# Moving the forget term, the third state and the gate of a transformer stage between VectorE, ScalarE and TensorE

## What is computed

```python
# shared_kv: once, from the state after layer 0
h = modulate(rms_norm(x, kv_norm_g), shift, scale)
kvf = h @ kv_w                                   # keys, values, 16 forget logits
k = rms_norm(k, k_norm_g)
dcum = cumsum(log_sigmoid(f_logit))              # [16 heads, 256]
# layer 1
h = modulate(rms_norm(x, pre_mix_g[1]), sh_m, sc_m)
qg = h @ w_qg                                    # q and gate
q = rms_norm(q, q_norm_g); gate = sigmoid(qg[..., 1024:])
logits = q k^T * scale + dcum[t] - dcum[s]       # causal
o = softmax(logits) v
y = (o * gate) @ w_o
```

## Time and profile before

| | |
|---|---|
| median of 3 runs | 1771.63 us (1769.91 to 1776.13) |
| the profiled execution | 1773.06 us, of which its span 1771.3 us |
| TensorE busy | 1724.3 us, 97% of the span |
| VectorE / ScalarE busy | 1149.1 us, 65% / 896.9 us, 51% |
| mean granted TensorE clock | 0.993 |
| bytes moved | 362.93 MB, 205 GB/s mean |

### The profile page before, as it was taken

How to read it: one execution, slowest core, us unless ns; L and a number is a source line. 1 busy time by engine, 2 the same in 40 slices (tenths; PEclk the granted TensorE clock), 3 DMA queues, 4 the chain that set the end, 5 groups by cost and what they waited for, 6 DMA issues and landing times.

```text
span 1771.3 us, 22292 instructions
## 1 busy us (share of the span) xinstructions
PE 1724.3 (97%) x9048; PEld 1436.2 (81%) x9048; DVE 1149.1 (65%) x1600; ACT 896.9 (51%) x1280; POOL 7.7 (0%) x21
## 2 busy tenths in 40 slices
PE   9999999999989999999999989999999999999998
PEld 6897788888767888888889858888888889778887
DVE  5888977788757654655457967554655556675553
ACT  4755544464667444544444566444544355574432
POOL 0000000000000000000000000000000000000000
PEclk9999999999999999999999999999999999999999
DMA  9958677856534655555564325545654565345451
GB/s 387 415 218 322 246 299 290 323 209 260 206 120 177 254 199 178 209 184 177 186 212 152 119 72 187 182 175 190 214 183 169 195 210 221 106 155 187 168 192 48
DMA packets 54840, 362.93 MB, mean 205 GB/s; under 512 B 5825, under 2 KB 9025, under 8 KB 14546
## 3 DMA queue, kind: packets, MB, share of 16 engines
q1 hardware_dynamic: 52978, 350.95, 54.1%
q0 software_dynamic: 1760, 10.56, 1.5%
HBM read 360.43 MB, written 1.05 MB: 204 GB/s over the span
## 4 chain that ended last, share of the span: by engine, by line
PE 77%; DVE 12%; ACT 2%; issue 1%; DMA 0%; DVEq 0%; ACTq 0%
PE pp L634 73%; DVE low L1924 4%; DVE raw L1937 2%; PE pp L909 2%; PE pp L841 1%; DVE hf L2068 1%; ACT wh L1381 1%; PE pp L986 1%; DVE tb L1924 0%; DVE hl L1924 0%; DVE x L1927 0%; DVE Sb L2219 0%; DVE sc L2320 0%; DVE h L1924 0%; DVE top L2317 0%
## 5 line engine op out<-in xcount | busy, mean ns | idle before, releaser
L1924 DVE TENSOR_TENSOR low<-raw,wh 128x2048 fp32r<-128x2048 f32 (+3 forms) x346 | 639.0, 1861 | 363.9 <-ACT wh L1381 363.4
L1381 ACT ACTIVATE wh<-raw 128x2048 fp32r<-128x2048 f32 (+3 forms) x352 | 536.9, 1544 | 421.6 <-PE pp L634 290.8
L634 PE MATMUL pp<-wh,hh 128*128 128x512 f32 x1312 | 521.7, 398 | 5.3 <-ACT hh L1648 2.2
L634 PE MATMUL pp<-low,hh 128*128 128x512 f32 x1312 | 510.1, 390 | 0.6 <-DVE low L1924 0.4
L634 PE MATMUL pp<-wh,hl 128*128 128x512 f32 x1312 | 506.9, 392 | 3.5 <-DVE hl L1924 3.5
L634 PEld LDWEIGHTS pp<-wh,hh 128*128 128x128 f32 x1312 | 247.5, 189 | 63.5 <-issue 11.9
L634 PEld LDWEIGHTS pp<-wh,hl 128*128 128x128 f32 x1312 | 247.2, 189 | 57.1 <-DVE hl L1924 4.7
L634 PEld LDWEIGHTS pp<-low,hh 128*128 128x128 f32 x1312 | 246.6, 188 | 50.1 <-DVE low L1924 1.7
L634 PE MATMUL pp<-wh,hidh 128*128 128x512 f32 x592 | 232.1, 392 | 0.0
L634 PE MATMUL pp<-wh,hidl 128*128 128x512 f32 x592 | 230.6, 389 | 0.0
L634 PE MATMUL pp<-low,hidh 128*128 128x512 f32 x592 | 230.5, 389 | 0.0
(11 more groups left out here) (230 smaller groups left out, 1187.0 us busy)
## 6 DMA issues: line engine op xcount, KB each, us to landing
raw<-in_w SPq DMA_DIRECT2D x300, 1024.0 KB, 4.8
raw<-in_w SPq DMA_DIRECT2D x24, 768.0 KB, 4.3
raw<-in_w SPq DMA_DIRECT2D x13, 512.0 KB, 19.2
firstw<-in_w SPq DMA_DIRECT2D x6, 1024.0 KB, 14.5
gain<-in_w POOLq DMA_DIRECT2D x6, 512.0 KB, 5.1
bT<-in_rel POOLq DMA_DIRECT2D x1, 2048.0 KB, 10.4
cst<-in_csts POOLq DMA_DIRECT2D x1, 1029.0 KB, 10.0
xT<-in_xT SPq DMA_DIRECT2D x1, 1024.0 KB, 5.5
```

The lines of the kernel that those rows point to most:

```text
L634: return e.matmul(out, lhsT, rhs, start=start, stop=stop, skip_group_check=True)
L1381: q.then_inc(e.activation(wh[j % NW][:, c], raw_of(i, kt * n)[:, c], ACT.Copy), s_wh, (j, part))
L1924: return e.tensor_tensor(out, a, b, op)
```

## The change

It does six things, all between the start of `kv_v` 0 and the end of this attention.

1. The high and low part of the forget sum lie in one tile (rows 0-31 and 64-95 high, 32-63 and 96-127 low), so a head needs one matmul of 64 rows instead of two of 32. `dL` and eight `dR` are made on ScalarE (9 instructions) instead of VectorE (10).
2. The third state is made on ScalarE from PSUM (16 instructions of 128 columns) instead of VectorE (8 of 512).
3. The sigmoid becomes exp(min(x,0) - ln(1 + exp(-|x|))): Abs (2), Exp, Ln, Exp on ScalarE, min (2) and a subtraction on VectorE; no change of table. The PSUM pair is released by the second min.
4. Four ada pieces each in three stretches of the stream instead of twelve evenly.
5. One more empty fill call after `q1`, and one after `gate1` (there ScalarE and VectorE have the first part of the sigmoid).
6. Two fill calls a round up to round 7 instead of 4.

```diff
-    marks = [..., (52, 32), (56, 32), (72, 44), (78, 44), (88, 48)]
+    marks = [..., (52, 32), (54, 32), (58, 36), (60, 36), (64, 40), (67, 40), (71, 44), (78, 44), (88, 48)]
...
         def fox_rate(i):
-            return 2 if i < 5 else 1
+            return 2 if i < 8 else 1
...  (TensorE: scores)
-                            rr = slice(32 * (h % 4), 32 * (h % 4) + 32)
-                            for i in range(2):
-                                ins = mm(s_r..., dL[i][rr, 128 * u["qb"]:128 * u["qb"] + 128],
-                                         dR[i][h // 4][rr, 0:nk], False, i == 1)
+                            rr = u["rows"]
+                            ins = mm(s_r..., dL[rr, 128 * u["qb"]:128 * u["qb"] + 128],
+                                     dR[h // 2][rr, 0:nk], False, True)
...  (TensorE: fox_fill)
                 yield from group("q1", 0, h(3), (s_side, ("qk", "q1")), fillp)
                 yield
+                yield
                 head_norm("q1", t_r)
                 yield "second"
-                yield from group("gate1", 0, h(3), (s_gate, ("gate", 1)), fillp)
+                yield from group("gate1", 0, h(3), (s_side, ("gate_min", 1, 1)), fillp)
+                yield
                 yield "own"
...  (ScalarE)
+            def gate_abs(g, ring):
+                _, before = ta.begin(("gate", g), (s_side, ("gate_less", g)))
+                q.wait_ge(*before)
+                q.wait_ge(s_mm, (("gate", "gate1")[g], 0, "end"))
+                for n in range(2):      # 128 x 512 each, PSUM -> a
+                    q.then_inc(e.activation(a[:, t, :], ring...tiles[:, t, :], ACT.Abs), s_sideact, ("gate_abs", g, n))
+            def gate_log(g):            # 128 x 1024 each
+                q.then_inc(e.activation(a, a, ACT.Exp, scale=-1.0), s_sideact, ("gate_exp", g))
+                q.then_inc(e.activation(a, a, ACT.Ln, bias=1.0), s_sideact, ("gate_log", g))
+            def gate_sigmoid(g):
+                q.wait_ge(s_side, ("gate_less", g))
+                q.then_inc(e.activation(o, o, ACT.Exp), s_gate, ("gate", g))
...  (ScalarE: fox_fill)
-                yield from ahead.steps("q1", 0, "T")
+                for n, _ in enumerate(ahead.steps("q1", 0, "T")):
+                    if n == 3:
+                        gate_sigmoid(0)
+                    yield
                 head_squares("q1", fillp)
                 yield
+                yield
                 head_roots("q1", t_r)
                 yield "second"
                 yield from ahead.steps("gate1", 0, "T")
-                gate_sigmoid(1, fillp)
+                gate_abs(1, fillp)
+                gate_log(1)
+                yield
                 waiting("fox", 4, gT)
                 yield "own"
+                gate_sigmoid(1)
...
+            def third_h(m):             # between the pieces of kv_k
+                for c in range(2):
+                    q.wait_ge(s_aux, ("hT", 3, m, c))
+                    for i in range(4):
+                        ins = e.activation(h3[:, m, k, :], misc...[:, 128 * i:128 * i + 128], ACT.Identity, bias=..., scale=...)
+                    q.then_inc(ins, s_h3, ("hf", 3, m, c))
+            def forget_sides():         # after values(("vv", 1)), ahead of group("q", 0)
+                e.activation(dL[:, :], dH[:, :], ACT.Identity, bias=fc[:, 1:2], scale=fc[:, 0:1])
+                for j in range(8):
+                    ins = e.activation(dR[j][:, :], dH[:, :], ACT.Identity, bias=fc[:, 10 + j:11 + j], scale=fc[:, 2 + j:3 + j])
+                q.then_inc(ins, s_sideact, "dR")
-            ahead.group("q", 0)
+            ahead.group("q", 0, upto=1)
             head_squares("q")
             ahead.first("gate", 0)
             head_roots("q")
-            gate_sigmoid(0, pairs)
+            gate_abs(0, pairs)
+            gate_log(0)
...  (VectorE)
+            gate_min(0, pairs) ahead of attention; in fox_fill gate_less(0) before the third call's yield,
+            gate_min(1, fillp) in the new call after gate1, gate_less(1) ahead of lo_of(4, 0..3)
-            ahead.group("kv_k", 0, between=lambda: h_parts(3, 0, *inputs_of("q")))   # and for 1
+            ahead.group("kv_k", 0)
-            q.then_inc(tt(dD[:, :], dT[:, :], dH[:, :], ALU.subtract), s_side, "dD")
-            for i, d in enumerate((dH, dD)):
-                e.tensor_scalar(dL[i][:, :], d[:, :], fc[:, 0:1], fc[:, 1:2], ALU.mult, ALU.add)
-                for j in range(4):
-                    ins = e.tensor_scalar(dR[i][j][:, :], d[:, :], ...)
+            for r in (slice(32, 64), slice(96, 128)):
+                q.then_inc(tt(dH[r, :], dT[r, :], dH[r, :], ALU.subtract), s_side, ("dD", r.start))
```

More of the change, by code:

```diff
@@ L175, in constants @@
     z = np.zeros((128, 128))
-    forget = np.zeros((128, 10))
+    forget = np.zeros((128, 18))
     forget[:, 0] = p % 32 < 16
     forget[:, 1] = p % 32 >= 16
-    for j in range(4):
-        for g in range(4):
-            forget[32 * g + 16 + 4 * j + g, 2 + j] = -1.0
-            forget[32 * g + 4 * j + g, 6 + j] = 1.0
+    for j in range(8):
+        for g in range(2):
+            for part in range(2):
+                forget[64 * g + 32 * part + 16 + 2 * j + g, 2 + j] = -1.0
+                forget[64 * g + 32 * part + 2 * j + g, 10 + j] = 1.0
     made = {"ident": np.eye(128),
@@ L352, in build @@
         lf = [place(f"lf{i}", [128, T], F32, big + 34816 + 1024 * i) for i in range(3)]
-        dH, dD = [place(f"d{n}", [128, T], F32R, big + 34816 + 1024 * i) for i, n in enumerate("HD")]
-        dL = [place(f"dL{i}", [128, T], F32R, big + 33792 - 1024 * i) for i in range(2)]
-        dR = [[place(f"dR{i}{j}", [128, T], F32R, big + o) for j, o in enumerate(places)]
-              for i, places in enumerate(((38912, 39936, 40960, 41984), (36864, 37888, 43008, 44032)))]
+        dH = place("dH", [128, T], F32R, big + 34816)
+        dL = place("dL", [128, T], F32R, big + 33792)
+        dR = [place(f"dR{j}", [128, T], F32R, big + 36864 + 1024 * j) for j in range(8)]
         aq = place("aq", [128, 4, T], F32, big)
@@ L1201, in tensor_program @@
             whole("q", 0, h(3), (s_side, ("qk", "q")))
-            whole("gate", 0, h(3), (s_gate, ("gate", 0)), between=lambda: head_norm("q"))
+            whole("gate", 0, h(3), (s_side, ("gate_min", 0, 1)), between=lambda: head_norm("q"))
             into_attention()
@@ L2256, in lo_of, with gate_min, gate_less @@
                 s_lo.at["h", hv, tile, 0] = s_lo.n
+            def gate_min(g, ring):
+                for n in range(2):
+                    t = slice(2 * n, 2 * n + 2)
+                    q.wait_ge(s_sideact, ("gate_abs", g, n))
+                    q.then_inc(e.tensor_scalar(gT[:, 4 * g + 2 * n:4 * g + 2 * n + 2, :],
+                                               ring.of((("gate", "gate1")[g], 0)).tiles[:, t, :], 0.0, None, ALU.min),
+                               s_side, ("gate_min", g, n))
+            def gate_less(g):
+                o = gT[:, 4 * g:4 * g + 4, :]
+                q.wait_ge(s_sideact, ("gate_log", g))
+                q.wait_ge(s_side, ("gate_min", g, 1))
+                q.then_inc(tt(o, o, ta.of(("gate", g))[:, :, :], ALU.subtract), s_side, ("gate_less", g))
             def split_fox(u):
@@ L2299, in fox_fill @@
             def fox_fill():
-                yield from ahead.steps("q1", 0, "T")
+                for n, _ in enumerate(ahead.steps("q1", 0, "T")):
+                    if n == 2:
+                        gate_less(0)
+                    yield
                 head_begin("q1")
+                yield
                 yield
@@ L2305, in fox_fill @@
                 yield from ahead.steps("gate1", 0, "T")
+                gate_min(1, fillp)
+                yield
+                gate_less(1)
                 for tile in range(4):
@@ L2529, in vector_program @@
             modulated("q")
-            ahead.group("kv_k", 0, between=lambda: h_parts(3, 0, *inputs_of("q")))
+            ahead.group("kv_k", 0)
             head_begin("kv_k0")
-            ahead.group("kv_k", 1, between=lambda: h_parts(3, 1, *inputs_of("q")))
+            ahead.group("kv_k", 1)
             head_begin("kv_k1")
@@ L2560, in vector_program @@
             head_scale("q", qg, qT[:, 0:4, :])
+            gate_min(0, pairs)
             fill = Fill(fox_fill())
```

41 lines of the change are left out of this document (27 added, 14 removed).

## The result

The changed kernel takes **1781.58 us** (median of 4 runs, 1780.88 to 1783.55), the kernel before in the same comparison 1773.06 (1769.91 to 1776.13). The ratio is 1.0045, 95% interval 1.003 to 1.0059: slower by 8 us. The forecast was 1773.5, in a range of 1763 to 1781. What came is the second rival (slower by the clock, 1779), 2.6 us above its price.

The account below looks back on a forecast made before the run. TensorE, busy 97%, was taken as the bound, with VectorE late at `q`. Attention +4.0, ahead of it -4.5 and half clock +1.7 gave net +1.2 on 1773.06, 1774.3, stated as 1773.5 us; range 1763 to 1781.

Parts of the forecast that it names:

- the second rival: Clock falls at all three long waits in attention (norm, round 9, `o`), 1.7 to 2.4 us each: 1779; chance 0.22.
- the price of the clock: In attention: one stretch at half clock counted, given idle stretches of 3.8 us, +1.7 us.
- The sum: Attention 78.0 us (57.3 work, 20.7 losses) against 74.0; ahead of it -4.5; clock +1.7; net +1.2, giving 1774.3.
- Ahead of attention: Before attention: VectorE relieved, `k_scale(0)` at about 420, both waits at `q` go, gate starts earlier: -4.5 us.
- the signs of being wrong: Observations that would refute the forecast: attention of 74 us or less, or a wait for low parts in `kv_k`.
- The stalls: Attention waits: 1.4 at start, 4.0 in rounds 3 to 5, 3.9 around the norm, 3.8 at round 9, 4.6 at `o`.
- The forget term: In attention: half of each four forget matmuls goes, 8 times each, -3.2 us; up to -4.8 if heads' matmuls overlap.
- The sigmoid: In attention: the new chain adds +1.1 us at the start and belongs to the +2.4 us at `o`.
- Rival 1: VectorE and ScalarE keep up, ada43 lands before it is missed, the gain stays: 1762 to 1765, say 1764; chance 0.24.

Follow-up runs that it names:

- The unread products: Changed kernel plus 78 extra matmuls of 256 columns, results unread, in four places where TensorE idles: 1774.08 us, ratio 0.9998 to the kernel before.
- the kernel with the work alone: Changed kernel with all three order edits undone (old ada marks, old rate, no empty steps): 1768.35 us, ratio 0.9966; another session 1769.35, 0.9975.

## Why the prediction was wrong

**The step that failed is the price of the clock.** The sum had "one as well, +1.7". Attention was put at 78.0 + 1.7 = 79.7 us and took 83.7. Split as above, the idle time was 18.3 us (I had 20.7), the work 57.1 (57.3), and the clock took up to 8.4. The unread products settle it: the same order with the clock held took 78.02 us. That is the sum's 78.0, with no fall counted. I had seen three of the places and their size, and had the case as a rival (three falls, 1779), but gave it 0.22. The fourth, the wait of 2.3 us at the turn of round 5, stood in the sum and not among the places where the clock might fall; it fell there as well, and twice as long at `o`. What spoke for it was in the sum itself: it held waits of 2.3, 3.8, 3.9 and 4.6 us where the trace of before had nothing longer than 2.15 in attention. In the changed kernel the clock fell behind every one of these four. The rule of the Trainium skill, "TensorE: Matmul & The Clock Gate", section "HAM oscillation", by which gaps between bursts bring it about each time, holds for these four waits, but not for the kernel before, which kept the clock through 2.15 and 2.83 us.

Of the 8.1 us between forecast and median, attention holds 4.0, the part ahead of it 0.9 and the part behind it 1.7. The other 1.5 are no step of the kernel: the median lies 0.7 above the profiled execution, and the forecast 0.8 below the sum's 1774.3. (By its own reason, 1.4 above the median, it should have been 1772.9.)

**Ahead of attention: right.** I said -4.5 us. It starts 3.56 us earlier, in an execution that was already 0.6 late in unedited work (the product ahead of the first low part starts at 384.06, before at 383.44): -4.2. `k_scale(0)` I had at 420 and full clock at `q`, and VectorE's timeline has it at 419.56; the new wait at `kv_k` 0 is 0.60 (0.7), that at `q` 0.81 (0.6). (A wait for low parts in `kv_k` also stood among the signs of being wrong; the sum itself has this one.)

```profile
419.56 1.28 DVE L1978 SCALAR_TENSOR_TENSOR kT<-pp,col,tb 128x1024 f32<-128x1024 f32 x1
```

ScalarE's nine instructions for the forget term took 4.6 us (I had 4.3), and the gate started with no wait.

**The stalls: right in place and cause, the long ones each within 0.8 us.** At the start 1.53 (1.4), round 5 2.23 (2.3), `gate1` 3.19 (3.9), round 9 3.99 (3.8), `o` 3.96 and 0.48 (4.6). Only those for the normalises of rounds 2 and 3 (0.23 and 0.28) were half or less of what I gave them. The moment of the first `gate1` step was missed, 480.20 instead of 478.2: attention started 0.9 later than forecast, and the norm's eight products ran at the lower clock (3.30 us; 1.96 with the clock held). VectorE's row for round 9 and ScalarE's for `o` show the two mechanisms that were forecast:

```profile
495.66 1.23 DVE L1988 CUSTOM_DVE_ANT_0 raw<-raw,cact 128x1024 f32<-128x1024 f32 x1 [5.69 <-DMA raw<-in_w]
...
498.68 0.48 DVE L2286 TENSOR_SCALAR Pb<-Pb,st 128x128 f32<-128x128 f32 x2
```

```profile
509.41 1.06 ACT L1626 ACTIVATE ta<-ta 128x1024 f32<-128x1024 f32 x1
510.50 1.06 ACT L1628 ACTIVATE ta<-ta 128x1024 f32<-128x1024 f32 x1
511.88 1.15 ACT L1385 ACTIVATE wh<-raw 128x512 fp32r<-128x512 f32 x2 [0.33 <-DMA raw<-in_w]
...
513.46 1.33 ACT L1668 ACTIVATE hh<-gT 128x256 fp32r<-128x256 f32 x4
```

But to be the last to end is not to be the only one late. With the ada pieces back in place, 3.19 of the 3.99 us stayed, as a weight piece then waited for the same buffer; with the logarithm out of the way, the wait for `hh` went and one of 2.76 came. At round 9 VectorE and ScalarE are not short of time (busy 4.27 and 3.50 us of the 10 from 490); what comes late is a buffer that TensorE itself frees, and with the old rate the wait behind it is 1.86. So there the long rate brings TensorE to the turn too early for the transfer.

**The forget term: too small.** I took -3.2 us, with -4.8 as the bound for an overlap, "as nothing in the trace shows an overlap". It is about -5.1. Of the kernel before, TensorE's timeline:

```profile
482.45 0.49 PE L634 MATMUL pp<-kT,qT 64*128 64x128 f32 x4
...
486.51 0.70 PE L634 MATMUL pp<-kT,qT 64*128 64x256 f32 x4
```

From the scores to the product behind the forget term it took 0.79 us (482.45 to 483.24) and 1.07 (486.51 to 487.58, both ends in the earlier trace rows); now it takes 0.48 (483.99 to 484.47) and, with the scores at 488.35, 0.74. That is 0.31 and 0.33, eight times each, 5.1 us. Part of it lies in the scores themselves: they took 0.42 and 0.63 us ahead of products of 32 rows, and take 0.24 and 0.34 ahead of those of 64. This fits the 63.7 us of work before and the 58.9 in the kernel with the work alone. I had counted the products and left out what stands ahead of them. That the work still came to the 57.3 us of the sum is luck: the 60.5 that I subtracted from was too low as well (63.7 by the split, good to about 2 us).

**The sigmoid: the sum had it as one loss among others.** Undoing it alone, in the old order, gives 3.3 us with an uncertainty of about 2; the sum's terms for it were +1.1 at the start and part of the +2.4 at `o`.

**After attention: 1.7 us that no step had.** 1.4 of them come behind the wait of 2.84 us at 1030.13, in work that the change does not touch: from there to the last transposition it takes 743.50 us, before 742.06. The stretch from 1030 shows 0.69, before 1.00; the kernel before has its 0.83 from 1050. With the unread products in attention it is 742.24, with 0.83 from 1020. The two executions of the new work in the old order, one program, take 742.26 and 743.64, and only the second shows the lower clock there (0.83 from 1020, 0.87 from 1050). So a difference of 1.4 us there comes between executions of one kernel; that it was chance in the changed kernel too is likely, but its other executions have no trace to show it.

**Rival 1** (the gain stays) was true of the work in part: 1768 to 1769 in the order of the kernel before, 1766 with the old sigmoid, where it had 1764. The order took it away.

The rule of the Trainium skill, "ScalarE: Activation LUTs", section "Rules for kernel authors", to add and multiply on VectorE and not on ScalarE, was weighed in the prediction. The measurement decides against it here: with 5.3 and 3.2 us of such work moved to ScalarE `k_scale(0)` came 3.25 us earlier, both waits at `q` went, and attention started earlier by 3.6 us.

## What to carry to other kernels

When a sum puts several stalls of over 2 us into a stretch that had none, count a stretch at half clock behind each (here about 1.7 us apiece, 3.4 behind the last). One row in which the clock held through such a wait is no promise: the same program can keep it in one execution and lose it in the next. An edit that moves work between engines and an edit that reorders steps should be timed apart: here the first was worth about 5 us and the second cost about 13. And a wait named for one late operation tells who was last; take that one away before you believe that the time will follow.

## What the runs showed of the hardware

The stream of the changed kernel's gate, TensorE's timeline:

```profile
437.57 0.64 PE L637 MATMUL pp<-hl,wh 128*128 128x256 f32 x4
438.05 0.64 PE L637 MATMUL pp<-hh,wh 128*128 128x256 f32 x4
```

- Two products of 64 rows and 256 columns that lie in different rows seem to run side by side: a second pair added 0.12 us, which is what a single product of 256 columns takes in a full stream (four from 437.57 to 438.05). At 128 columns a second pair added 0.12 us as well, so there the rows show no such gain.
- Four score products of 64 rows and 128 columns gave way to the next product after 0.42 us when that had 32 rows, and after 0.24 when it had 64 (256 columns: 0.63 and 0.34).
- Products that nobody reads, put into the waits, kept the granted clock at 1.00 (78 of them in four waits, attention 83.7 to 78.0 us). 12 of them in one wait took away the lower clock behind that wait, cost nothing and gained nothing: in that execution the clock fell behind a wait of 1.55 us instead.
- Waits of 1.5 to 3 us bring the lower clock in some executions of one program and not in others: 0.98 and 0.95 in attention, 1.6 us apart; over the span 0.995 and 0.992, 5.1 us apart.
